# A hybrid decoder layer in 96 weight blocks: small transfers on SyncE, gate roots in the next round, later transposes and levels, another order of the last blocks

## The chip, the cores and the metric

The kernel runs on one core of a Trainium2 chip. The metric is device time in microseconds; lower is better. Names of the engines below: PE or TensorE (matmul), DVE or VectorE, ACT or ScalarE, POOL or GpSimd, SP or SyncE (here only a queue for DMAs).

## What is computed

One layer over 2064 prompt tokens (16 meta tokens in front of 2048) and 32 sample tokens (8 sequences of 4), width 1024, float32:

```python
u = rmsnorm(x, ln_mix) @ w_in                # 1024 -> 6*512: xa, ga, qb, fb, ib, gb
xc = conv_b + sum(xpad[:, j:j+T]*conv_w[j] for j in range(4))     # causal convolution of xa
r, ig = sigmoid(xc @ w_ra + b_ra), sigmoid(xc @ w_rx + b_rx)      # per head of 64
a = exp(-8 * r * softplus(-lam)); b = sqrt(1 - a*a) * ig * xc
h = scan(a*h + b);  y_a = h * gelu(ga)                            # group A
f = lb + (1-lb)*sigmoid(fb); k = (1-lb)*sigmoid(-fb); q = silu(qb)/sqrt(128); v = ib
S_t = f_t * S_{t-1} + k_t v_t^T ; o_t = q_t S_t                   # group B, 4 heads, in chunks
y_b = rms(o) * gn * silu(gb)
x = x + concat(y_a, y_b) @ w_out
x = x + square(relu(rmsnorm(x, ln_mlp) @ w_up)) @ w_down          # 1024 -> 4096 -> 1024
y = rmsnorm(x, ln_final)
```

The outputs are y and the new states (h, the last three xa, S) of the prompt and of each sample sequence.

## The kernel before

Everything lies transposed: features on the 128 partitions, tokens along the columns. The tokens are cut into two **passes** (p = 0, 1) of 1024 and 1072 columns; the second holds 1040 prompt columns and the 32 of the samples. A pass is cut into tiles of columns (`TILES`): two of 512 in pass 0, three of 358, 358 and 356 in pass 1. The weights are 96 **blocks** of 1024 x 128, kept split in two float32r parts, w_hi (rounded by ScalarE, `round_weights`) and w_lo = w_st - w_hi (by GpSimd's `split` or by VectorE, L1438). Two blocks are on chip at a time (slot = block mod 2). In pass 0 SyncE loads each block and stores its parts to DRAM (`load`, `keep`), in pass 1 GpSimd's queue loads the parts back (`reload`, L448, L449).

A **unit** is one block by one tile: 8 row blocks x 3 matmuls (w_hi a_hi, w_hi a_lo, w_lo a_hi; L481 to L483) into one of four PSUM banks (`bank`). VectorE reads the bank out and frees it. Blocks 0 to 19 are the four heads' V, G, XA, F, Q (one head is a **round**), 20 to 23 are GA, 24 to 31 OUT (the output projection), 32 to 95 the MLP. The activations are split likewise: `turn` makes a_hi (ScalarE) and a_lo (VectorE, L1189) of the mixer's output for OUT.

In blocks 0 to 23 each unit is issued in two halves; a half is a **slot** of `schedule(p)`. A round of pass 0 has 20 slots, of pass 1 30; the last round, over GA, has 16 and 24. Behind a slot's half unit every engine runs the **pieces** that the tables give that slot, mostly for the head before (i-1), each in the same order in its own queue:

- VT, KT: transposes of v and k. D and L1 to L7: products inside a chunk at distance levels; VectorE multiplies q and k by decays between levels (`merge`, L1151 to L1154), places results by mask. U: state updates. O: outputs of the head; R, N: the reciprocal and the scaling of its norm; OT: transposes back; Y: times gate, into `xy`. OT opens aux PSUM banks (four, numbered in turn by `AUX`), as do the others.
- GATE: products for r and ig and ScalarE's sigmoids, exp, tanh. GA: VectorE's u, a, v, igx from them, and ScalarE's square root of v. GB: VectorE's product with the root and the scan (L1297 to L1306).
- RS: the sums of squares of the input, its root and reciprocal (L1122). No bank can be read out before it. NF, FN, FY: the final norm of pass 0's output, run within pass 1's first round. TURN: `turn` of an early tile.

ScalarE issues the small transfers of a pass (`load_small`: masks, h0, convolution history; `load_state`) before its first slot, the state stores and loads within O, small outputs at the end of the rounds, and the loads of the residual x. VectorE waits for the small transfers before RS. OUT's first `SIDE` = 4 units run their first six row blocks, then their last two (the last heads are ready last). At the end, `FINAL_ORDER` puts blocks 94 and 95 (rows m = 6, 7) by tile: (6,0) (7,0) (6,1) (7,1) (6,2) (7,2); `last_sum` adds the residual and squares, `final_sum` sums a tile over partitions on TensorE, `finish_tile` inverts (L1122) and scales its eight row blocks (L1132), and SyncE stores them.

Of the kernel before, what the change touches and what calls it, by code (L numbers as in the profile page):

```python
# [35 lines left out]
HEADS = 4  # L36
# [27 lines left out]
SIDE = 4  # L64
# [21 lines left out]
def y_no(p, t, n):  # L86
# [7 lines left out]
               + [(m, t) for t in range(NT[1]) for m in (KB - 2, KB - 1)]]  # L94
# [37 lines left out]
def s_at(p, i, name):  # L132
# [18 lines left out]
def schedule(p):  # L151

    out = []
    for i in range(HEADS + 1):
        blks = [5 * i + b for b in range(5)] if i < HEADS else [GA0 + c for c in range(4)]
        s = 0
        for blk in blks:
            for t in range(NT[p]):
                for half in range(2):
# [5 lines left out]
                    if i >= 1 and s in SLOTS[p]:  # L165
                        pieces.append((SLOTS[p][s], i - 1))
                    if i < HEADS and s == GATE_SLOT[p]:
                        pieces.append(("GATE", i))
# [11 lines left out]
def aux_uses(p, name):  # L180

    if name in ("FN", "FY", "R", "N", "Y", "GA", "GB", "TURN"):
        return 0
    if name in ("RS", "N2", "NF"):
        return NT[p]
    if name == "GATE":
        return 2 * NT[p]
# [22 lines left out]
AUX = number_aux()  # L210


def build(nc, ins, outs):
# [6 lines left out]
    with ExitStack() as ctx:  # L220
# [170 lines left out]
        def _(sync):  # L391
# [10 lines left out]

            load(0, 0)
# [7 lines left out]
            sync.dma_start(w_rx[:, :, :], wrx_d).then_inc(const_in, 16)  # L411
            with sync.Fori(0, BLOCKS // 2 - 1) as i:
                for j in range(2):
                    sync.wait_ge(w_ready, 2 * i + (j + 1))
                    load(2 * i + (2 + j), j)
                    keep(2 * i + j, j)
            for j in range(2):
                sync.wait_ge(w_ready, BLOCKS - 1 + j)
                keep(BLOCKS - 2 + j, j)
            for t, (c0, w) in enumerate(KEPT[1]):  # L420
# [5 lines left out]
        def _(pool):  # L426
# [13 lines left out]
            for j in range(2):  # L440
                split(j, j)
# [22 lines left out]
        def _(pe):  # L464
# [40 lines left out]
            def piece(p, name, i):  # L505
# [115 lines left out]
                elif name == "GATE":  # L621
# [3 lines left out]
                    for t, (c0, w) in enumerate(TILES[p]):  # L625
                        for g, wt in enumerate((w_ra, w_rx)):
                            ps = open_bank(a + 2 * t + g)
# [8 lines left out]
            for p in range(2):  # L636
                nt = NT[p]

                for it, blk, t, half, pieces in schedule(p):
# [8 lines left out]
                    for name, i in pieces:  # L648
                        if name not in ("FN", "FY", "R", "N", "Y", "GA", "GB", "TURN"):
# [8 lines left out]
                for m, t in units[:SIDE]:  # L658
# [64 lines left out]
            for m, t in FINAL_ORDER[1][-2 * NT[1]:]:  # L723
# [4 lines left out]
                if t and m == KB - 2:  # L728
                    final_sum(1, t - 1)
# [5 lines left out]
        def _(act):  # L735
# [44 lines left out]

            def load_small(p):

                for b in range(P // BLK):
                    r_ = slice(BLK * b, BLK * (b + 1))
                    act.dma_start(mask[r_, 0:BLK], mask_d[0:BLK, 0:BLK]).then_inc(smp_in, 16)
                    act.dma_start(mask[r_, BLK:].rearrange("p (l j) -> p l j", j=HALF),
                                  mask_d[0:BLK, P:P + 64 * (DIRECT - 1)].rearrange(
                                      "p (l j) -> p l j", j=64)[:, :, 0:HALF]).then_inc(smp_in, 16)
                if p == 0:
                    return  # L790
                for g, (s0, w) in enumerate(blocks(NCH)):
                    act.dma_start(smask[s0:s0 + w, :], smask_d[s0:s0 + w, SGRP * g:SGRP * (g + 1)]).then_inc(smp_in, 16)
                act.dma_start(h0[:, :, :], h0_d).then_inc(smp_in, 16)
                act.dma_start(spad[:, :, :, 0:TAPS - 1], cs_d).then_inc(smp_in, 16)

            def load_state(i):
                act.dma_start(s_smp[:, :, :], ss_d[i]).then_inc(s_load, 16)
# [33 lines left out]
            def piece(p, name, i):  # L831
# [7 lines left out]
                elif name == "FY":  # L839
                    act.wait_ge(y_out, i + 1)  # L840
                    store(0, i, META, TH[0] - META)
# [47 lines left out]
                elif name == "O":  # L889
# [13 lines left out]
                    if p and i + 1 < HEADS:  # L903
                        act.wait_ge(s_step, s_at(p, i, "smul"))
                        load_state(i + 1)
                    if p:
                        for s in (3, 4):
                            drained(act, AUX[(p, "U", i)] + s)
                        act.dma_start(ssn_d[i], tmp[:, :, :]).then_inc(s_store, 16)
# [11 lines left out]
                elif name == "GATE":  # L921
# [3 lines left out]
                    for t, (c0, w) in enumerate(TILES[p]):  # L925
                        for g, (dst, b) in enumerate(((ta, "b_ra"), (ig, "b_rx"))):
                            u = a + 2 * t + g
                            filled(act, u)
                            fn(dst[:, c0:c0 + w], aux[u % 4][:, 0:w], ACT.Sigmoid,
                               bias=col(b, i)).then_inc(aux_free[u % 4], 1)  # L930
                    for t in range(NT[p]):
                        drained(act, a + 2 * t)
# [3 lines left out]
                elif name == "GA":  # L936
# [38 lines left out]
            for p in range(2):  # L975
# [675 lines left out]
```

## Time and profile before

| | |
|---|---|
| median of 3 runs | 2451.21 us (2449.23 to 2453.65) |
| profiled execution | 2453.71 us, its span 2451.8 us |
| PE busy | 2385.6 us, 97% of the span |
| DVE, ACT, POOL busy | 38%, 26%, 12% |
| mean granted TensorE clock | 0.988 |
| chain that ended last | PE 87%, DVE 7%, issue 3%, ACT 2% |

The span is the time from the first to the last instruction in the profiled execution; 1.9 us lie around it. A wait is idle time of an engine, put down to what ended it. Pass 0's projections run up to about 375 us, its OUT blocks to about 476, its MLP to about 1175; pass 1's projections to about 1576.

### The profile page before, as it was taken

Reading aid. Unit: us, or ns where it says so; the run is one execution under the profiler, and the core shown is the slowest. Engines: PE = TensorE matmul, PEld = TensorE weight load, DVE = VectorE, ACT = ScalarE, POOL = GpSimd, SP = SyncE. Lnnn points to the kernel's source line nnn. Section 1 sums busy time; section 2 is a strip of 40 time slices with the busy share of each in tenths; the row PEclk is TensorE's granted clock in tenths of the full one; section 3 lists DMA queues with packets and bytes.
Section 4 is the critical chain, followed back from the end, with each engine's and each line's share of the span. In section 5 each row is a group of like instructions: output and inputs, shape, how many; then the busy total and the mean of one; then the engine's idle time right before and its main releaser. Section 6 shows DMA issues by size and latency. Waiting matters only on the chain.

```text
span 2451.8 us, 38616 instructions
## 1 busy us (share of the span) xinstructions
PE 2385.6 (97%) x15850; PEld 2140.7 (87%) x15850; DVE 937.6 (38%) x1593; ACT 645.6 (26%) x1207; POOL 287.1 (12%) x276
## 2 busy tenths in 40 slices
PE   7999998999999999999999999999999999999996
PEld 5777776888888888888898899999999999999996
DVE  6766664421121121223775665544212212211224
ACT  5345343331131121222334234422201201200211
POOL 0000002222122221222000000000001000010000
PEclk9999998999999999999999999999999999999998
DMA  5332324344434444454432222332222322222223
GB/s 200 106 112 100 107 96 175 133 155 147 153 132 153 141 141 154 134 200 156 126 109 70 70 70 87 120 122 86 86 86 89 99 87 86 86 90 98 86 86 106
DMA packets 88178, 284.39 MB, mean 116 GB/s; under 512 B 15872, under 2 KB 19072, under 8 KB 88064
## 3 DMA queue, kind: packets, MB, share of 16 engines
q1 hardware_dynamic: 46512, 158.09, 18.7%
q0 software_dynamic: 27648, 100.68, 12.3%
q10 hardware_dynamic: 13904, 23.95, 2.8%
q8 instruction: 90, 1.47, 0.2%
q14 instruction: 24, 0.20, 0.0%
HBM read 171.06 MB, written 111.62 MB: 115 GB/s over the span
## 4 chain that ended last, share of the span: by engine, by line
PE 87%; DVE 7%; issue 3%; ACT 2%; ACTq 1%; DMA 0%; POOL 0%; DVEq 0%; POOLq 0%
PE bank L481 27%; PE bank L483 27%; PE bank L482 27%; PE aux L628 1%; PE aux L548 1%; DVE a_lo L1197 1%; DVE xc L1380 1%; ACT s_in L737 1%; PE aux L577 1%; PE aux L600 1%; PE aux L599 1%; ACT w_hi L737 0%; DVE xy L1306 0%; DVE rs L1141 0%; DVE xy L1132 0%
## 5 line engine op out<-in xcount | busy, mean ns | idle before, releaser
L481 PE MATMUL bank<-a_hi,w_hi 128*128 128x358 f32 (+3 forms) x2560 | 924.1, 361 | 32.1 <-DVE a_lo L1197 11.3
L482 PE MATMUL bank<-a_lo,w_hi 128*128 128x358 f32 (+3 forms) x2560 | 907.2, 354 | 0.0
L483 PE MATMUL bank<-a_hi,w_lo 128*128 128x358 f32 (+3 forms) x2560 | 907.2, 354 | 0.0
L481 PEld LDWEIGHTS bank<-a_hi,w_hi 128*128 128x128 f32 x2560 | 486.3, 190 | 84.5 <-POOL w_lo L436 19.0
L483 PEld LDWEIGHTS bank<-a_hi,w_lo 128*128 128x128 f32 x2560 | 486.9, 190 | 43.6
L482 PEld LDWEIGHTS bank<-a_lo,w_hi 128*128 128x128 f32 x2560 | 486.8, 190 | 42.7 <-issue 1.5
L481 PE MATMUL bank<-b_hi,w_hi 128*128 128x358 f32 (+3 forms) x1280 | 450.2, 352 | 0.0
L482 PE MATMUL bank<-b_lo,w_hi 128*128 128x358 f32 (+3 forms) x1280 | 449.2, 351 | 0.0
L483 PE MATMUL bank<-b_hi,w_lo 128*128 128x358 f32 (+3 forms) x1280 | 449.0, 351 | 0.0
L1508 DVE TENSOR_TENSOR xy<-xy,bank 128x356 f32 (+6 forms) x160 | 94.0, 588 | 556.1 <-PE bank L483 556.1
L737 ACT ACTIVATE a_hi<-tmp 128x356 f32 (+5 forms) x160 | 88.3, 552 | 817.3 <-DVE tmp L1498 817.3
L436 POOL TENSOR_TENSOR w_lo<-w_st,w_hi 128x1024 fp32r<-128x1024 f32 x74 | 183.8, 2484 | 975.8 <-ACT w_hi L737 975.8
L483 PEld LDWEIGHTS bank<-b_hi,w_lo 128*128 128x128 f32 x1280 | 240.8, 188 | 20.7
L482 PEld LDWEIGHTS bank<-b_lo,w_hi 128*128 128x128 f32 x1280 | 240.3, 188 | 20.7 <-issue 0.2
L481 PEld LDWEIGHTS bank<-b_hi,w_hi 128*128 128x128 f32 x1280 | 240.3, 188 | 19.9 <-issue 0.2
L1498 DVE SCALAR_TENSOR_TENSOR tmp<-bank,rs 128x356 f32<-128x356 f32 (+2 forms) x160 | 94.6, 591 | 332.1 <-PE bank L483 331.2
L448 POOL DMA_DIRECT2D w_hi<-kept_hi x96 | 50.9, 530 | 1139.2 <-PE bank L483 1139.2
L737 ACT ACTIVATE w_hi<-w_st 128x1024 fp32r<-128x1024 f32 x96 | 100.8, 1050 | 276.5 <-PE bank L483 267.9
L1501 DVE TENSOR_TENSOR a_lo<-tmp,a_hi 128x356 f32 (+5 forms) x160 | 95.1, 595 | 197.9 <-ACT tmp L737 197.9
L737 ACT ACTIVATE tmp<-tmp 128x356 f32<-128x356 f32 (+2 forms) x160 | 85.7, 536 | 0.0
L737 ACT ACTIVATE tmp<-xy 128x496 f32<-128x496 f32 (+2 forms) x75 | 40.8, 544 | 147.3 <-DVE xy L1508 147.1
L737 ACT ACT_TABLE_LOAD x57 | 73.1, 1283 | 6.5 <-issue 5.5
(166 smaller groups left out, 1407.5 us busy)
## 6 DMA issues: line engine op xcount, KB each, us to landing
w_st<-in_wall SPq DMA_DIRECT2D x96, 512.0 KB, 4.1
kept_hi<-w_hi SPq DMA_DIRECT2D x96, 512.0 KB, 4.9
kept_lo<-w_lo SPq DMA_DIRECT2D x96, 512.0 KB, 5.7
w_hi<-kept_hi POOLq DMA_DIRECT2D x96, 512.0 KB, 3.8
w_lo<-kept_lo POOLq DMA_DIRECT2D x96, 512.0 KB, 4.6
xs<-in_xT ACTq DMA_DIRECT2D x8, 536.0 KB, 7.7
xy<-in_xT ACTq DMA_DIRECT2D x8, 536.0 KB, 8.3
xy<-in_xT ACTq DMA_DIRECT2D x8, 512.0 KB, 8.2
```

Source lines behind the costliest of these rows:

```text
L436: pool.tensor_tensor(w_lo[:, slot, :], w_st[:, slot, :], w_hi[:, slot, :].bitcast(F32), ALU.subtract).then_inc(w_ready, 1)
L448: pool.dma_start(w_hi[:, slot, :], kept_hi[m]).then_inc(w_again[slot], 16)
L481: pe.matmul(ps, wh, xh, start=(j == 0), stop=False)
L482: pe.matmul(ps, wh, xl, start=False, stop=False)
L483: mm = pe.matmul(ps, wl, xh, start=False, stop=(j == 7))
L548: mm = pe.matmul(ps[s0:s0 + w, HALF * c:HALF * (c + 1)], k[:, at:at + w], right_halves(q, at, w, x), start=True, stop=True)
L577: mm = pe.matmul(ps[:, j * P:(j + 1) * P], k_tok[0:r_, c + j, :], v_tok[0:r_, c + j, :], start=True, stop=True)
L599: pe.matmul(out, q[:, lo_:hi_], s_in[:, c + j, :], start=True, stop=False)
L737: return nc.scalar.activation(out, in_, func, **kw)
L1498: stt(z, bank[lu % 4][:, 0:w], 0.0, rs[:, c0:c0 + w], ALU.max, ALU.mult).then_inc(bank_free[lu % 4], 1)
L1501: tt(a_lo[:, 4 * qd + j, c0:c0 + w], z, a_hi[:, 4 * qd + j, c0:c0 + w].bitcast(F32), ALU.subtract).then_inc(h_ready, 1)
L1508: tt(x, x, bank[lu % 4][:, 0:w], ALU.add).then_inc(bank_free[lu % 4], 1)
```

## The change

- SyncE gets `load_small`, `load_state`, the state stores, the small outputs, the stores of pass 0's output (FY) and, in pass 1, the loads of the residual x. `load_small(0)` stands before SyncE's weight loop, all else after it.
- A new piece GS holds ScalarE's square root of v, at slot 0 of the next round; GB stays at slot 0 (pass 0) and 1 (pass 1). GA goes from slot 27 to 28 in pass 1.
- Pass 0: L1 to N one slot later (D stays), OT from 14 and Y from 15 both to 16, GATE from 16 to 15, RS from 7 to 6. Pass 1: OT from 21 and Y from 22 both to 25; GATE's first two tiles from slot 24 to 23, its third as GATE2 at 24; NF, FN, FY three slots later. In the last round OT and Y are at 15 (pass 0) and 22, 23 (pass 1).
- GpSimd splits blocks 0 to 4 instead of 0 and 1; VectorE splits 5 to 23 instead of 2 to 23.
- `SIDE` is 3 in pass 0. `round_weights(25)` comes before `turn` of the second tile.
- The last blocks run (6,0) (6,1) (7,0) (7,1) (6,2) (7,2), and the final sums and scalings are placed anew.

The diff, cut to its core; its hunks are in the order constants, SyncE, GpSimd, ScalarE, VectorE.

```diff
-SIDE = 4
+SIDE = [3, 4]
+DVE_FIRST = 5
...
-               + [(m, t) for t in range(NT[1]) for m in (KB - 2, KB - 1)]]
+               + [(KB - 2, 0), (KB - 2, 1), (KB - 1, 0), (KB - 1, 1), (KB - 2, 2), (KB - 1, 2)]]
+SUM_AT = {(KB - 1, 1): 0, (KB - 2, 2): 1}
...
-SLOTS = [dict(zip(range(16), PIECES)),
-         dict(zip([0, 4, 5, 6, 8, 9, 10, 12, 13, 14, 15, 16, 18, 19, 21, 22], PIECES))]
-GATE_SLOT = [16, 24]
-GATE_A_SLOT, GATE_B_SLOT = [18, 27], [0, 1]
+AT = [[0, 1] + list(range(3, 15)) + [16, 16],
+      [0, 4, 5, 6, 8, 9, 10, 12, 13, 14, 15, 16, 18, 19, 25, 25]]
+AT_LAST = [AT[0][:-2] + [15, 15], AT[1][:-2] + [22, 23]]
+GATE_SLOTS = [{15: "GATE"}, {23: "GATE", 24: "GATE2"}]
+GATE_TILES = [{"GATE": [0, 1]}, {"GATE": [0, 1], "GATE2": [2]}]
+GATE_A_SLOT, GATE_ROOT_SLOT, GATE_B_SLOT = [18, 28], [0, 0], [0, 1]
...
-RS_SLOT = [7, 1]
-FINAL_SLOTS = {6: ("NF", 0), 7: ("FN", 0), 8: ("FN", 1), **{10 + b: ("FY", b) for b in range(8)}}
+RS_SLOT = [6, 1]
+FINAL_SLOTS = {9: ("NF", 0), 10: ("FN", 0), 11: ("FN", 1), **{13 + b: ("FY", b) for b in range(8)}}
...
+            load_small(0)
             with sync.Fori(0, BLOCKS // 2 - 1) as i:
...
+            sync.wait_ge(unit_done, unit_no(0, BLOCKS - KB, 0))
+            load_small(1)
+            sync.wait_ge(x_acc, 2 * KB)
+            sync.wait_ge(x_ready, tile_no(1, NT[1] - 1, KB - 1))
+            load_state(0)
+            for b in range(KB):
+                sync.wait_ge(y_out, b + 1)
+                sync.dma_start(y_d[b, :, META:TH[0]], xy[:, b, META:TH[0]]).then_inc(stored, 16)
+            for i in range(HEADS):
+                for s in (3, 4):
+                    drained(sync, AUX[(1, "U", i)] + s)
+                sync.dma_start(ssn_d[i], tmp[:, :, :]).then_inc(s_store, 16)
+                if i + 1 < HEADS:
+                    filled(sync, AUX[(1, "O", i)] + 2)
+                    sync.wait_ge(s_step, s_at(1, i, "smul"))
+                    load_state(i + 1)
+            sync.wait_ge(rg_step, rg_at(1, 3, "ncs"))
...
-            for j in range(2):
-                split(j, j)
+            for n in range(DVE_FIRST):
+                split(n % 2, n)
...
-                elif name == "GA":
+                elif name == "GS":
                     act.wait_ge(rg_step, rg_at(p, i, "v"))
                     fn(ea[:, 0:TH[p]], ea[:, 0:TH[p]], ACT.Sqrt, scale=-1.0).then_inc(rg_act, 1)
...
-                turn(p, NT[p] - 1, range(EARLY))
                 if p == 0:
                     round_weights(OUT0 + 1)
+                turn(p, NT[p] - 1, range(EARLY))
...
-                    if p == 0 and 0 < blk < OUT0 - 1 and t == 0 and half == 0:
+                    if p == 0 and DVE_FIRST - 1 <= blk < OUT0 - 1 and t == 0 and half == 0:
...
-                if t and m == KB - 2:
-                    finish_tile(t - 1, range(3))
-                elif t and m == KB - 1:
-                    finish_tile(t - 1, range(3, KB))
+                if (m, t) == (KB - 1, 1):
+                    finish_tile(0, range(5))
+                elif (m, t) == (KB - 2, 2):
+                    finish_tile(0, range(5, KB))
+            finish_tile(1, range(KB))
             finish_tile(NT[1] - 1, range(KB))
```

## Rows read from the trace of the kernel before

**Rows 1.** The page, part 5, groups: busy us, mean ns of one | idle before.

```profile
L436 POOL TENSOR_TENSOR w_lo<-w_st,w_hi 128x1024 fp32r<-128x1024 f32 x74 | 183.8, 2484 | 975.8 <-ACT w_hi L737 975.8
...
L737 ACT ACT_TABLE_LOAD x57 | 73.1, 1283 | 6.5 <-issue 5.5
```

**Rows 2.** Waits of TensorE over the span: us in total, times, longest.

```profile
PE aux L619 <- ACT s_in L737: 9.3, 13, 2.3
PE bank L481 <- POOL w_lo L436: 7.1, 2, 4.0
PE bank L481 <- DVE v L1340: 6.2, 1, 6.2
PE aux L498 <- ACT rs L737: 5.1, 1, 5.1
PE aux L498 <- DVE gate L1531: 4.6, 2, 3.3
PE bank L481 <- DMA w_lo<-kept_lo: 3.8, 1, 3.8
PE aux L548 <- DVE q L1216: 2.4, 4, 0.6
...
PE bank L481 <- DVE w_lo L1438: 2.0, 1, 2.0
PE bank L481 <- DVE a_lo L1189: 1.8, 2, 1.1
```

**Rows 3.** Stretches of TensorE: us, PE busy (count), granted clock, DMA share, GB/s.

```profile
41.44:48.27 6.83, 4.96 (x12) 0.50 0.55 200
386.19:393.02 6.83, 5.85 (x14) 0.50 1.02 390
...
430.00:436.83 6.83, 6.83 (x32) 1.00 0.44 176
1195.14:1201.97 6.83, 4.75 (x12) 0.50 0.53 85
1314.61:1318.02 3.41, 3.41 (x13) 0.50 0.02 5
1399.94:1406.77 6.83, 6.64 (x23) 0.50 0.00 0
...
1700.00:1706.83 6.83, 6.83 (x44) 1.00 0.39 134
2410.29:2417.12 6.83, 5.55 (x19) 0.50 0.01 3
```

**Rows 4.** Timeline of ScalarE and VectorE, start of pass 0: start us, us, instruction [idle before].

```profile
32.95 0.34 ACTq L785 DMA_DIRECT2D mask<-in_mask  x1
...
36.77 1.06 ACT L737 ACTIVATE w_hi<-w_st 128x1024 fp32r<-128x1024 f32 x1 [5.33 <-issue]
...
39.10 3.35 DVE L1122 RECIPROCAL rs<-rs 128x512 f32<-128x512 f32 x1
```

**Rows 5.** Timeline of TensorE and GpSimd at OUT; of VectorE late in pass 0.

```profile
383.69 0.40 PE L483 MATMUL bank<-a_hi,w_lo 128*128 128x512 f32 x1
387.17 0.78 PE L481 MATMUL bank<-a_hi,w_hi 128*128 128x496 f32 x1 [3.08 <-POOL w_lo L436]
...
381.04 6.08 POOL L436 TENSOR_TENSOR w_lo<-w_st,w_hi 128x1024 fp32r<-128x1024 f32 x1 [12.42 <-ACT w_hi L737]
...
1160.67 1.10 DVE L1531 TENSOR_TENSOR gate<-gate,tmp 128x496 f32<-128x496 f32 x1 [0.69 <-ACT tmp L737]
...
1171.58 0.68 DVE L1531 TENSOR_TENSOR gate<-gate,tmp 128x496 f32<-128x496 f32 x1 [0.68 <-ACT tmp L737]
```

**Rows 6.** Timeline of TensorE and VectorE, start of pass 1.

```profile
1191.12 0.99 PE L498 MATMUL aux<-gate,ones 128*128 128x496 f32 x2
...
1198.20 2.39 DVE L1122 RECIPROCAL rs<-rs 128x358 f32<-128x358 f32 x1 [10.37 <-DMA spad<-in_conv]
```

**Rows 7.** Timeline of VectorE, last instructions of the kernel.

```profile
2444.83 4.09 DVE L1132 SCALAR_TENSOR_TENSOR xy<-xy,par,gate 128x356 f32<-128x356 f32 x8
```

More of the change, by code:

```diff
@@ L164, in schedule @@
                         pieces.append(("RS", 0))
[L165 to L168, printed above, removed]
+                    if i >= 1 and s == GATE_ROOT_SLOT[p]:
+                        pieces.append(("GS", i - 1))
+                    if i >= 1:
+                        at = (AT if i < HEADS else AT_LAST)[p]
+                        pieces += [(name, i - 1) for name, slot in zip(PIECES, at) if slot == s]
+                    if i < HEADS and s in GATE_SLOTS[p]:
+                        pieces.append((GATE_SLOTS[p][s], i))
                     if i < HEADS and s == GATE_A_SLOT[p]:
@@ L185, in aux_uses @@
         return NT[p]
-    if name == "GATE":
-        return 2 * NT[p]
+    if name in ("GATE", "GATE2"):
+        return 2 * len(GATE_TILES[p][name])
     if name == "D" or name[0] == "L":
@@ L210, with gate_aux @@
 AUX = number_aux()
+def gate_aux(p, i, t):
+    name = "GATE" if t < 2 else "GATE2"
+    return AUX[(p, name, i)] + 2 * (t % 2)
 def build(nc, ins, outs):
@@ L401, in load_x0, with load_small, load_state @@
                 sync.dma_start(xs[:, b, c0:c0 + w], xT[b, :, c0:c0 + w]).then_inc((x_in2 if t else x_in)[b], 16)
+            def load_small(p):
+                for b in range(P // BLK):
+                    r_ = slice(BLK * b, BLK * (b + 1))
+                    sync.dma_start(mask[r_, 0:BLK], mask_d[0:BLK, 0:BLK]).then_inc(smp_in, 16)
+                    sync.dma_start(mask[r_, BLK:].rearrange("p (l j) -> p l j", j=HALF),
+                                  mask_d[0:BLK, P:P + 64 * (DIRECT - 1)].rearrange(
+                                      "p (l j) -> p l j", j=64)[:, :, 0:HALF]).then_inc(smp_in, 16)
+                if p == 0:
+                    return
+                for g, (s0, w) in enumerate(blocks(NCH)):
+                    sync.dma_start(smask[s0:s0 + w, :], smask_d[s0:s0 + w, SGRP * g:SGRP * (g + 1)]).then_inc(smp_in, 16)
+                sync.dma_start(h0[:, :, :], h0_d).then_inc(smp_in, 16)
+                sync.dma_start(spad[:, :, :, 0:TAPS - 1], cs_d).then_inc(smp_in, 16)
+            def load_state(i):
+                sync.dma_start(s_smp[:, :, :], ss_d[i]).then_inc(s_load, 16)
             load(0, 0)
@@ L620, in piece @@
                         mm.then_inc(aux_done, 1)
-                elif name == "GATE":
+                elif name in ("GATE", "GATE2"):
                     if n == 0:
@@ L657, in _ @@
                 units = [(m, t) for m in range(KB) for t in range(nt)]
-                for m, t in units[:SIDE]:
+                for m, t in units[:SIDE[p]]:
                     if t == 0:
@@ L662, in _ @@
                     out_unit(m, t, range(EARLY))
-                for m, t in units[:SIDE]:
+                for m, t in units[:SIDE[p]]:
                     out_unit(m, t, range(EARLY, KB))
-                for m, t in units[SIDE:]:
+                for m, t in units[SIDE[p]:]:
                     if t == 0:
@@ L779, in input_squares @@
                     input_square(p, b)
[L781 to L797, printed above, removed]
             def rms_tile(p, a, dst, t, tiles):
@@ L920, in piece @@
                     turn(p, i, range(EARLY))
-                elif name == "GATE":
+                elif name in ("GATE", "GATE2"):
                     if i > 0:
@@ L1463, in _ @@
                     for name, i in pieces:
-                        if name not in ("RS", "NF", "GATE"):
+                        if name not in ("RS", "NF", "GATE", "GATE2", "GS"):
                             piece(p, name, i)
```

71 lines of the change are left out of this document (30 added, 41 removed).

## The prediction

> **What bounds the kernel now.** I read the page first, then the waits of TensorE, then its low-clock stretches by the timeline, then the timelines of the other engines around each long wait. TensorE is busy 97% of the span and its matmuls are the same in both kernels: the products of w_hi, w_lo with the activations, plus the small ones of the heads. So only three things can move the time: waits of TensorE, stretches in which its clock is granted at 1.2 instead of 2.4 GHz, and the tail after its last product. [Rows 2] names the waits: nearly all are single events at seams (start of a pass, last projection round, OUT products, end) or recur once in each head's round. [Rows 3] shows the stretches at half clock; each begins in or right behind a wait of 2 us and more. Their price comes from the counts: at full clock a 512-column product starts every 6.83/30 = 0.23 us (32 are counted, two lie over the ends), a 358-column one every 6.83/42 = 0.16; in the slow stretches 5.85/14 = 0.42 and 5.55/19 = 0.29. So a product in such a stretch costs 0.19 us more in pass 0 and 0.13 more in pass 1 [rows 3]. A wait costs more than its printed idle time as well: the last product before the wait at 387.17 starts at 383.69, 3.48 later stands the next, against 0.23 usual, so 3.25 are lost where 3.08 are printed [rows 5]: 0.17 more for each wait.
>
> **Start of pass 0** (small transfers to SP, `RS` one slot earlier, GpSimd splits blocks 0 to 4). Before, ScalarE issues eight mask transfers from 32.95 on and rounds block 2's weights only at 36.77; the square roots and VectorE's reciprocal, at 39.10, stand behind [rows 4], and TensorE waits 6.2 us for the V read-out [rows 2]. On SP the eight issues, 3.8 us (36.77 - 32.95), come before its loop, where SP's next need, the third weight load, isn't wanted by ScalarE before about 33: hidden; if not, it is the same 3.8. Rounding then starts at about 32.95, and TensorE's sums of squares can run there too (the same x_acc releases both; TensorE, a half unit earlier in its order, waits there for about 0.5). The w_lo split leaves VectorE too, so the reciprocal starts at about 34.8 and the bank comes free 4.4 earlier: 1.8 of the 6.2 stay. The slow stretch of 12 products goes: 12 x 0.19 = 2.3. Term: 4.4 + 2.3 = **6.7**. The later wait of 2.0 for VectorE's w_lo (L1438, behind convolution and `rest_of_prep`) goes, as GpSimd makes block 4's half: its 2.48 us [rows 1] have most of a block's products, 48 x 0.23 = 11 us, as cover. Term: **2.0**.
>
> **The rounds of pass 0.** Levels stand a half unit later behind D. L1 waited for D's VectorE work 2.4 us in four waits [rows 2]; the extra half unit is 12 x 0.23 = 2.8 us: gone. The gate roots (`GS`) go from slot 18 to the next round's slot 0. Before, ScalarE stood at slot 18 until VectorE had v, with every later instruction behind it; now its root, about as long as a rounding of that width (1.06, [rows 4]; an estimate), and a table load of 1.28 [rows 1] stand in front of V's copies, and VectorE's `GB` (product and scan) waits for them with its bank read-outs queued behind. I bound this between -1.3 (one table switch less before the round) and +2.3 us on VectorE's side; near zero is likeliest, as the root moves past one sigmoid only, and the 2.8 of the shifted levels covers either end. Term: **2.4**.
>
> **The transposes of OT, both passes.** They waited 9.3 us in 13 waits, the longest 2.3 [rows 2]: in pass 1 the norm N sits behind the convolution on VectorE and arrives at its slot late. Now OT comes two slots after N in pass 0 (5.6 us) and six after it in pass 1 (six half units, 12 us, against two). All 9.3 go. The three slow stretches behind them, 13, 23 and again 13 products (the third, at 1488.69, is as the first), go with them: 49 x 0.13 = 6.4. Term: **15.7**. OT now opens aux banks that the gates just used; TensorE waits there if ScalarE's sigmoids lag. `GATE2` splits the pass-1 set so that four products, not six, come at once, with a half unit between: bounds 0 to 1 us a round in pass 1, taken 0.3.
>
> **OUT of pass 0.** Two waits for GpSimd's w_lo, 7.1 in all, and 0.7 of the 1.8 for a_lo L1189 [rows 2]. The first w_lo took 6.08 us [rows 5] against 2.48 on average [rows 1], while VectorE ran its a_lo subtractions back to back. Moved ahead of `turn`, the rounding ends about 1.1 earlier than the first a_hi, so GpSimd starts before that run. Its mirror image is in the trace: with a split in flight, VectorE's subtraction-like tensor_tensor at 1160.67 takes 1.10 where the same at 1171.58 takes 0.68 [rows 5]. So whoever starts first keeps the other out: w_lo of block 25 takes 2.5 and is in time, the first a_lo of the second tile comes about 1.4 late, of which the shift of the last round (OT no longer ahead of the last products) hides half. I leave 0.8 of wait. That is the reading of the Trainium skill, page "SBUF — State Buffer", section "SBUF: two separate sides", too: the port pair shared by VectorE and GpSimd is an exclusive lock that the first to start keeps for its whole instruction; the trace agrees by 1.10 against 0.68. SIDE = 3 puts unit (1,1) whole, 24 x 0.23 = 5.5 us, between the end of block 24 and the use of block 26, in place of two quarter units (2.8): the 4.0 wait goes. Both slow stretches, 14 products each (the second one at 406.67 is like the first), go: 28 x 0.19 = 5.3. Term: 7.1 + 0.7 - 0.8 + 5.3 = **12.3**. If GpSimd is starved once more, as in the row of 6.08, w_lo comes 1.9 late and a slow stretch follows: 12.3 - 4 = 8.
>
> **Start of pass 1.** ScalarE issued twelve small transfers and the state load before the square roots; VectorE's reciprocal waited 10.4 us for the last to land [rows 6] and TensorE 5.1 for the root [rows 2]. On SP they follow the last `keep`, 20 us ahead. The reciprocal can then start at 1187.9 (1198.20 - 10.37), TensorE has products for its fourth bank until 1191.12 at least and half a unit more with NF out of the way, and the first bank is free by 1187.9 + 2.4 + 0.5 (a read-out, about as wide as a scaling) = 1190.8 [rows 6]: no wait. NF to slot 9 keeps aux banks out of it. Slow stretch: 12 x 0.13 = 1.6. Term: **6.7**. What is late next is VectorE, with two reciprocals, eight output scalings (now slots 13 to 20) and the convolution before gate slot 23: I allow 0 to 2 us, in the small waits below.
>
> **End of pass 1's rounds.** ScalarE issues five small outputs before the third `turn`; on SP they cost it nothing. The 1.1 left of a_lo L1189 goes: **1.1**. SP is idle there; its queue holds state stores, state loads and residual loads in the order in which they fall due, half a round and more ahead of each use: nothing.
>
> **The end.** Block 95's reload is 3.8 us late [rows 2], with a slow stretch of 19 x 0.13 = 2.5 behind. The new order puts (6,1) in front of (7,0): 24 x 0.16 = 3.9 us of cover, just enough (0 to 0.3 stays). Of the 4.6 for the last sums the first, 1.3, goes too. With 0.17 for each restart TensorE ends 8 us earlier. But all eight scalings of tile 1 and its reciprocal now come after the last sum, where five stood: 2.4 + 3 x 0.51 = 3.9 more on VectorE (0.51 = 4.09/8, [rows 7]). Term: 8.2 - 3.9 = **4.3**.
>
> **Sum.** 6.7 + 2.0 + 2.4 + 15.7 + 12.3 + 6.7 + 1.1 + 4.3 = 51.2. Restarts: 23 waits outside the tail x 0.17 = 3.9. New small waits (gates, VectorE's load, a table load at the wrong place): -2.6, taken between 0 and 6. Together -52.5 us. The profiled span of 2451.8 becomes 2399.3; that run took 2453.7, 2.5 above the median of 2451.2, so the run would be 2401.2 and the median 2451.2 - 52.5 = **2398.7 us**.
>
> **Rivals.**
> (a) Waits shrink below what is printed but clock stretches stay at several seams, since a rest of 1 to 2 us is left there: start, OUT and two of the rounds, 2.3 + 5.3 + 3.4 plus their rests of 4: 2411 to 2414. For it: 1.8 and 0.8 are left by my own sum. Against: waits of 2.0 (L1438) and 1.1 had no slow stretch behind them.
> (b) OT's new place moves the wait instead of removing it (the change doesn't do what it says): TensorE then waits for ScalarE's gate sigmoids by as much as it did for N. Term 15.7 lost: 2414.
> (c) The roots at the round's start are on the path: a table load and root, 2.3, per round, with a slow stretch of 1.7 to 2.5 behind: seven rounds x 4 to 4.8 = 28 to 34: 2427 to 2433.
> (d) Slower than before: the same place, but VectorE, waiting in GB, holds its read-outs until all four banks are full. A round then loses the root, the covered 2.8 of the levels, and up to a unit (5.5 in pass 0) with its slow stretch: about 10 us, x 7 = 70: 2469. It decides against the change from 57/7 = 8.2 us a round. Against it: four banks are three units of slack, 12 to 16 us.
>
> **How the numbers follow.** My forecast, 0.76: 2390 to 2408. (a) 0.12, (b) 0.05, (c) 0.03, (d) 0.02, and 0.02 for other small gains or none. The range of 8 in 10 takes the forecast's bounds and reaches into (a) and (b): 2388 to 2416. Faster by over 0.2% (about what a measurement of this kernel can tell from no change, 5 us): 0.96; within: 0.02; slower: 0.02.
>
> **What would show it.** TensorE's waits without L1438, the q of L1216, POOL w_lo, DMA w_lo, and s_in; the clock granted in full at 1195, in the rounds of pass 1 and near the last blocks; GpSimd's second OUT split near 2.5 us and VectorE's first a_lo beside it longer than 0.6; ScalarE without DMA issues at both pass starts; the last sum near 8 us earlier relative to block 89's end and 13 us of VectorE behind it. I'd be wrong if aux L619 or L628 waits for ScalarE's sigmoids, if VectorE waits for ea in GB with TensorE idle, or if new waits of over 2 us stand at the seams.

## The result, and the profile after

The changed kernel takes 2426.68 us (median of 4 runs, 2424.64 to 2428.21) against 2452.43 of the kernel before (4 runs, 2449.23 to 2453.84): ratio 0.9896, 95% interval 0.9879 to 0.9913. The direction was right, the size was half of the forecast: 25.7 us less where 52.5 were predicted, and 2426.68 lies above the range of 2388 to 2416. The profiled execution took 2426.67, its span is 2425.0 (before 2451.8), so the two traces differ by 26.8.

The page of the kernel after, its head and parts 1 and 4:

```profile
span 2425.0 us, 38626 instructions
...
PE 2375.2 (98%) x15850; PEld 2137.6 (88%) x15850; DVE 936.9 (39%) x1590; ACT 642.7 (27%) x1207; POOL 291.7 (12%) x279
...
PE 93%; DVE 3%; ACT 1%; issue 0%; DVEq 0%; ACTq 0%
```

Its waits of TensorE, the view of [rows 2]: us in total, times, longest. Line numbers have moved: L540 to L542 are the products (L481 to L483 before), L658 the product of O, L607 the levels, L594 D, L557 the sums of squares, L1209 `turn` of the mixer's output (L1189).

```profile
PE aux L658 <- DVE s_in L1274: 14.4, 4, 4.7
PE bank L540 <- DVE a_lo L1217: 11.1, 1, 11.1
PE bank L540 <- DVE a_lo L1209: 3.1, 1, 3.1
PE aux L557 <- DVE gate L1550: 2.8, 1, 2.8
PE aux L607 <- DVE q L1236: 1.9, 1, 1.9
PE bank L540 <- DVE v L1359: 1.5, 1, 1.5
PE aux L594 <- DVE q L1374: 1.2, 1, 1.2
```

Gone are both w_lo waits of GpSimd, w_lo of L1438, the late reload, rs, all 13 of s_in from ScalarE (OT) and 4.7 of the 6.2 for v. The 11.1 is the first load of the kernel, before any product; the kernel before has it too. The first line is new and the largest: O waits for VectorE's state update U. The wait for a_lo of L1209 has grown: 3.1 in one, where two came to 1.8. On the page PE's busy time fell by 10.4 us (fewer products at half clock) and its share of the last chain rose from 87 to 93%.

The rows that answer [rows 4] and [rows 6], timeline of ScalarE and VectorE in the kernel after, starts of pass 0 and pass 1 (start us, us, instruction, idle before):

```profile
32.96 1.06 ACT L797 ACTIVATE w_hi<-w_st 128x1024 fp32r<-128x1024 f32 x1 [1.51 <-DVE rs L1161]
...
35.29 3.35 DVE L1142 RECIPROCAL rs<-rs 128x512 f32<-128x512 f32 x1 [2.37 <-ACT rs L797]
...
1188.14 2.39 DVE L1142 RECIPROCAL rs<-rs 128x358 f32<-128x358 f32 x1
```

Block 2's rounding is 3.8 us earlier (36.77 before), the reciprocal also (39.10 before; the prediction said 34.8), and pass 1's reciprocal no longer waits for a transfer.

Stretches of TensorE in the kernel after, the view of [rows 3]: length, busy time and count of PE, PEld, DVE, ACT, POOL, then the granted clock, DMA share and GB/s.

```profile
129.77:136.60 6.83, 5.65 (x26) 5.65 (x27) 2.40 (x5) 1.14 (x8) 0.00 (x0) 0.50 0.43 118
211.69:218.52 6.83, 6.11 (x28) 6.11 (x29) 2.04 (x4) 1.14 (x8) 0.00 (x0) 0.50 0.49 145
293.61:297.02 3.41, 2.93 (x13) 2.94 (x14) 1.83 (x3) 0.00 (x0) 0.00 (x0) 0.50 0.17 16
389.18:396.01 6.83, 6.14 (x15) 4.83 (x16) 5.93 (x10) 2.73 (x6) 0.00 (x0) 0.50 0.81 249
1180.00:1186.83 6.83, 6.83 (x39) 6.19 (x37) 6.70 (x15) 5.75 (x13) 0.00 (x0) 1.00 0.16 57
1532.65:1536.06 3.41, 3.41 (x15) 3.41 (x14) 2.79 (x5) 0.00 (x0) 0.00 (x0) 0.50 0.02 5
```

The stretch at the start of pass 1 (1180) now has the full clock, as predicted. Three new ones at 1.2 GHz stand in the rounds of pass 0, each from the last 0.5 to 1.2 us of one of O's waits on. One stands at the wait for a_lo (before, two at OUT), and one, at 1532.65, has no wait in front of it.

**Where the 26.8 went.** I took each product's start minus the start of the product before it, less the median of that spacing for the same pair of shapes, and summed the excess over each stage. That counts waits, what they cost beside their printed time, and slow stretches alike.

| stage | before | after | moved | forecast |
|---|---|---|---|---|
| start of pass 0 (to 60 us) | 10.7 | 4.7 | -6.0 | -6.7 |
| rounds of pass 0 (60 to 370) | 24.3 | 39.0 | **+14.8** | -6.6 |
| OUT of pass 0 | 14.5 | 6.4 | -8.1 | -12.3 |
| start of pass 1 | 7.4 | 0.7 | -6.7 | -6.7 |
| rounds of pass 1 | 28.8 | 13.5 | -15.3 | -14.6 |
| last blocks, to TensorE's end | 11.6 | 3.3 | -8.3 | -8.2 |
| from there to the kernel's end | 11.3 | 14.6 | +3.3 | +3.9 |

The forecast of 15.7 for OT is for both passes. Of the 9.3 us of its waits, seven (0.2 to 0.4 each, 2.2 in all) stood in pass 0, so 2.2 of it stand with the rounds of pass 0 (2.4 + 2.0 + 2.2 = 6.6) and 13.5 with those of pass 1. The stages sum to 26.3 (forecast 51.2, and 1.3 more for restarts less new small waits). One stage holds 21.4 of the miss of 26.2, OUT 4.2; the other stages are within 0.7 each.

**The new wait.** Timeline of VectorE in the kernel after, second round of pass 0 with an earlier head in it:

```profile
203.17 0.69 DVE L1359 TENSOR_TENSOR xpad<-bank,rs 128x512 f32<-128x512 f32 x1 [4.55 <-PE bank L542]
...
205.01 3.92 DVE L1399 SCALAR_TENSOR_TENSOR xc<-xpad,par,xc 128x1024 f32<-128x1024 f32 x3
208.97 0.23 DVE L1262 COPY s_in<-state 128x128 f32<-128x128 f32 x1
209.30 3.05 DVE L1274 SCALAR_TENSOR_TENSOR s_in<-s_in,f,aux 128x128 f32<-128x128 f32 x7
...
212.41 0.80 PE L658 MATMUL aux<-s_in,q 128*128 128x128 f32 x2 [4.71 <-DVE s_in L1274]
```

And VectorE at the same place of the kernel before:

```profile
206.19 0.35 DVE L1254 SCALAR_TENSOR_TENSOR state<-s_in,f,aux 128x128 f32<-128x128 f32 x1
206.69 0.69 DVE L1340 TENSOR_TENSOR xpad<-bank,rs 128x512 f32<-128x512 f32 x1 [0.15 <-PE bank L483]
...
208.54 3.93 DVE L1380 SCALAR_TENSOR_TENSOR xc<-xpad,par,xc 128x1024 f32<-128x1024 f32 x3
```

In pass 0 XA (the third block of a round) ends with slot 11, and there VectorE runs the read-out and the whole convolution, 5.8 us from 203.17 to 208.97, ahead of the slot's pieces. Before, U stood at slot 10: its chain was done at 206.54, and the read-out at 206.69 and the convolution stood behind it. With "L1 to N one slot later" U is at slot 11, behind the convolution, and O at slot 12 asks for it one half unit later. The last round projects GA and has no XA. U and O are at slots 11 and 12 there too, and O's wait is 0.2 us. That is a control inside the same trace:

```profile
369.74 0.49 PE L658 MATMUL aux<-s_in,q 128*128 128x128 f32 x2 [0.20 <-DVE s_in L1274]
```

### The profile page after: what moved, and what is told of

Read it like the earlier page. It is cut to its first block, busy times and chain, and to the rows that moved or that the text cites. A ratio compares the mean times of both kernels' runs of the same rounds, so it can differ in the third digit from the quotient of the medians.

```text
span 2425.0 us, 38626 instructions
## 1 busy us (share of the span) xinstructions
PE 2375.2 (98%) x15850; PEld 2137.6 (88%) x15850; DVE 936.9 (39%) x1590; ACT 642.7 (27%) x1207; POOL 291.7 (12%) x279
## 4 chain that ended last, share of the span: by engine, by line
PE 93%; DVE 3%; ACT 1%; issue 0%; DVEq 0%; ACTq 0%
PE bank L540 29%; PE bank L542 29%; PE bank L541 29%; PE aux L607 1%; PE aux L688 1%; PE aux L658 1%; PE aux L659 1%; DVE xc L1399 0%; DVE xy L1152 0%; DVE s_in L1274 0%; PE aux L613 0%; PE aux L636 0%; PE aux L557 0%; PE aux L626 0%; DVE gate L1142 0%
## 5 line engine op out<-in xcount | busy, mean ns | idle before, releaser
L540 PE MATMUL bank<-a_hi,w_hi 128*128 128x358 f32 (+3 forms) x2560 | 919.4, 359 | 15.8 <-DVE a_lo L1217 11.1
L542 PE MATMUL bank<-a_hi,w_lo 128*128 128x358 f32 (+3 forms) x2560 | 902.5, 353 | 0.0
L540 PEld LDWEIGHTS bank<-a_hi,w_hi 128*128 128x128 f32 x2560 | 482.1, 188 | 64.7 <-POOL w_lo L495 11.4
L542 PEld LDWEIGHTS bank<-a_hi,w_lo 128*128 128x128 f32 x2560 | 483.2, 189 | 43.3
L540 PE MATMUL bank<-b_hi,w_hi 128*128 128x358 f32 (+3 forms) x1280 | 450.2, 352 | 0.0
L542 PE MATMUL bank<-b_hi,w_lo 128*128 128x358 f32 (+3 forms) x1280 | 449.0, 351 | 0.0
L542 PEld LDWEIGHTS bank<-b_hi,w_lo 128*128 128x128 f32 x1280 | 240.8, 188 | 20.6
L540 PEld LDWEIGHTS bank<-b_hi,w_hi 128*128 128x128 f32 x1280 | 240.2, 188 | 19.9 <-issue 0.2
```

What stands on the lines that cost most here:

```text
L540: pe.matmul(ps, wh, xh, start=(j == 0), stop=False)
L542: mm = pe.matmul(ps, wl, xh, start=False, stop=(j == 7))
```

## The experiments

My theory (A) was: the new place of U and O behind XA's convolution costs some 22 us, three waits with their slow stretches; the rest of the miss lies at OUT. The rival (B): the loss hangs on the levels' shift or the moved roots as such, not on the convolution. Runs of e1 to e4 share one set of runs of before (median 2451.18), e5 to e8 a second (2450.65), e9 and e10 a third (2451.73).

**e4: the kernel before, with the level shift alone.**

```diff
-SLOTS = [dict(zip(range(16), PIECES)),
-         dict(zip([0, 4, 5, 6, 8, 9, 10, 12, 13, 14, 15, 16, 18, 19, 21, 22], PIECES))]
+AT = [[0, 1] + list(range(3, 15)) + [15, 15],
+      [0, 4, 5, 6, 8, 9, 10, 12, 13, 14, 15, 16, 18, 19, 21, 22]]
...
```

> The kernel before with one part of the change alone: L1 to N of pass 0 one slot later (OT and Y at 15), nothing else. Theory A: three waits of O of about 4.7 us appear with slow stretches behind, less the 2.4 us of L1's waits: about 19 us above the kernel before's 2452.4, 2471. Theory B: the shift alone does no harm, 2449 to 2453.

Measured: 2464.67 us, ratio 1.0058 (1.0041 to 1.0074), 13.5 us slower. Its waits of TensorE:

```profile
PE aux L599 <- DVE s_in L1254: 14.4, 4, 4.7
...
PE aux L619 <- ACT s_in L737: 6.8, 6, 2.0
```

The three waits and three stretches at half clock (133.76, 215.68, 297.60) come with this edit alone, and L1's waits go. So one part of the change, by itself, costs 13.5 us. I expected 19. My sum had counted only L1's 2.4 as a gain. The traces have more: pass 0's seven waits of OT (2.2), the four for k (0.9) and one of 0.8 are gone as well, 3.9 in all (OT too is one slot later here). That leaves 1.6 of the 5.5, about what a restart of 0.17 for each of these twelve waits makes (2.0).

**e2: the changed kernel, with the convolution of a round that has pieces put behind the slot's pieces.**

```diff
-                            convolve(p, un[0])
+                            if p == 0 and un[0] > 0:
+                                late = un[0]
+                            else:
+                                convolve(p, un[0])
...
+                    if late is not None:
+                        convolve(p, late)
```

> The changed kernel, all slots as changed, but in pass 0's second to fourth round VectorE runs the convolution behind the pieces of slot 11 (behind U) instead of ahead of them. Theory A: the three O waits fall below 0.5 us and the slow stretches in these rounds go, 22 us below the changed kernel: 2405; the gates' wait for the convolution stays hidden (their slot is 15). Theory B (roots at the round's start): U still comes late, gain under 3 us, 2424 or more. Theory C (moving the convolution only hands the wait on to GATE or to bank read-outs): O's waits go, as long ones of L688 or of L540 appear, 2415 to 2427.

Measured: 2403.24 us, 0.9811 (0.9795 to 0.9828), 23.4 less than the changed kernel. VectorE in that slot:

```profile
195.26 0.69 DVE L1359 TENSOR_TENSOR xpad<-bank,rs 128x512 f32<-128x512 f32 x1 [4.55 <-PE bank L542]
195.86 0.22 DVE L1262 COPY s_in<-state 128x128 f32<-128x128 f32 x1
196.20 3.07 DVE L1274 SCALAR_TENSOR_TENSOR s_in<-s_in,f,aux 128x128 f32<-128x128 f32 x7
199.37 0.35 DVE L1274 SCALAR_TENSOR_TENSOR state<-s_in,f,aux 128x128 f32<-128x128 f32 x1
```

The convolution follows; O's waits fall from 14.4 to 0.2 us, and all slow stretches between 60 and 360 us are gone. The levels and roots stand where the change put them, so (B) falls. No new wait of the gates (L688) or for a bank appears, so the wait isn't handed on (theory C). The two profiled executions are 24.6 us apart. By the excess of each product, 22 of it lie in these rounds: 14.6 of waits (3 x 4.88) and 7.3 in the three slow stretches. Most of the rest are a shorter stretch at OUT (3.41 for 6.83 us, 1.3) and the stretch at 1532.65, which e2's trace lacks (some 1.6); these two aren't the convolution's.

**e1: the levels back, the rest of the change kept.**

```diff
-AT = [[0, 1] + list(range(3, 15)) + [16, 16],
+AT = [list(range(14)) + [16, 16],
```

> The changed kernel with the pieces L1 to N of pass 0 back in their old slots (levels 2 to 8, KT 9, U 10, O 11, R 12, N 13); all else as changed. Theory A: the new 4.9 us waits of O for VectorE's s_in come from U standing in slot 11, in which VectorE convolves first, and from nothing else: the three waits (14.4 us) and their three slow-clock stretches (about 7) go, the waits of L1 for D's q (2 to 3 us in all) come back: about 19 us below the changed kernel's 2426.7, 2408. Theory B: VectorE is late in every round because the gate roots stand at the round's start: the O waits stay with L1 back, 2424 to 2428.

Measured: 2423.25 us, 0.9891 (0.9874 to 0.9907): (A) as I then had it, 2408, fell. O's waits and their stretches were gone, as (A) says, but the waits of TensorE have a new head:

```profile
PE aux L607 <- DVE q L1236: 12.6, 4, 4.7
```

The timelines of VectorE and TensorE at one of them show why:

```profile
165.98 1.23 DVE L1316 TENSOR_TENSOR k_tok<-k_tok,ea 128x1024 f32<-128x1024 f32 x1 [1.07 <-ACT ea L797]
167.25 2.35 DVE L1325 TENSOR_TENSOR_SCAN xy<-ta,hprev,k_tok 128x1024 f32<-128x1024 f32 x1
...
170.63 1.22 DVE L1236 TENSOR_TENSOR q<-q,f 128x1024 f32<-128x1024 f32 x1
...
171.90 0.74 PE L607 MATMUL aux<-q,k 128*32 128x16 f32 x64 [2.64 <-DVE q L1236]
```

ScalarE's root (ea) reaches `GB` 1.07 us late, behind a rounding and a table load; product and scan follow, and V's read-out and D's q stand behind them. L1 waits 2.6 in each of three rounds and 4.7 in the first, 0.6 at the longest before [rows 2]. So with the levels at their old slots VectorE's D is about 2 us later for TensorE than before. The wait for the root is 1.07 of that; what makes the rest isn't separated, since no run has both the levels and the roots at their old places. With the levels shifted these three waits are gone: the shift hides them, and the order of U and the convolution takes more than it gives.

**e3: the root back at slot 18 (28 in pass 1), the rest kept.** The piece GS is issued in the same round as GA.

> The changed kernel with the gate root back right behind GA in both passes (slots 18 and 28) instead of slot 0 of the next round. Theory A: O's waits of 4.7 us stay; the root's place is worth little: within 3 us of the changed kernel, 2424 to 2430. Theory B (roots at the round's start make VectorE late): O's waits shrink by 2 us each or go, 2405 to 2418.

Measured: 2424.59 us, 0.9893 (0.9877 to 0.991), within the spread of the changed kernel. O's waits stay at 14.4; the first round's L1 wait falls from 1.9 to 0.8, D's rises from 1.2 to 1.5. With the shift as cover the root's place is worth nothing that can be told here.

**The OUT seam.** The kernel after, timelines of VectorE, GpSimd and TensorE:

```profile
380.92 3.61 DVE L1209 TENSOR_TENSOR a_lo<-xy,a_hi 128x496 fp32r<-128x496 f32 x6 [3.06 <-ACT a_hi L797]
384.44 0.68 DVE L1359 TENSOR_TENSOR xc<-bank,rs 128x512 f32<-128x512 f32 x1
...
386.43 1.40 DVE L1302 SCALAR_TENSOR_TENSOR xy<-aux,par,gate 128x512 f32<-128x512 f32 x2
...
386.81 2.36 POOL L495 TENSOR_TENSOR w_lo<-w_st,w_hi 128x1024 fp32r<-128x1024 f32 x1 [16.95 <-ACT w_hi L797]
...
387.75 6.76 DVE L1209 TENSOR_TENSOR a_lo<-xy,a_hi 128x512 fp32r<-128x512 f32 x9
...
389.87 0.77 PE L540 MATMUL bank<-a_hi,w_hi 128*128 128x512 f32 x1 [3.10 <-DVE a_lo L1209]
```

GpSimd's split is in time (6.08 us in [rows 5], now 2.36), and VectorE's first a_lo of the second tile stands behind it: it takes 1.97 us (387.75 to 389.72), the others 0.68. Four runs on top of e2 took this apart.

*e5: the rounding of block 25 behind `turn` again.*

```diff
+                turn(p, NT[p] - 1, range(EARLY))
                 if p == 0:
                     round_weights(OUT0 + 1)
-                turn(p, NT[p] - 1, range(EARLY))
```

> The kernel of e2 (2403.2) with block 25's rounding back behind turn of the second tile. There TensorE waits 3.1 us for VectorE's first a_lo of that tile, which takes 2.0 us in place of 0.6 since GpSimd's split runs beside it. Theory L (the split and the subtractions of VectorE keep each other out, first come first): that wait falls to about 1.8 (what is left is VectorE's run on the first tile and Y), GpSimd's split takes about 6 us again and TensorE waits 3 to 3.5 for it, with the slow stretch: 2404 to 2408. Theory R (it is only ScalarE's 1.05 us rounding ahead of a_hi): the wait falls by 1.05 to 2.0 and nothing new comes: 2401 to 2402.

Measured: 2404.13 us, 0.9813 (0.9796 to 0.9829). The same instructions, GpSimd and VectorE:

```profile
367.81 6.09 POOL L495 TENSOR_TENSOR w_lo<-w_st,w_hi 128x1024 fp32r<-128x1024 f32 x1 [20.07 <-ACT w_hi L797]
...
365.62 6.06 DVE L1209 TENSOR_TENSOR a_lo<-xy,a_hi 128x512 fp32r<-128x512 f32 x10
```

The wait for a_lo falls from 3.1 to 1.8, and one of 1.5 for w_lo takes its place (I had expected 3 to 3.5): nothing gained. Rounding first costs VectorE 1.3 us (7.36 in e2 against 6.06 for ten a_lo) and gives GpSimd 3.7 (6.09 against 2.36). Of the 6.09, 2.2 lie behind the end of VectorE's run, nearly all that the split needs by itself.

*e6: the split of block 25 in four quarters of 256 columns.*

```diff
+            for c in range(4):
+                part = slice(DM // 4 * c, DM // 4 * (c + 1))
+                ins = pool.tensor_tensor(w_lo[:, 1, part], w_st[:, 1, part], w_hi[:, 1, part].bitcast(F32),
+                                         ALU.subtract)
...
```

> The kernel of e2 with GpSimd's split of block 25 cut into four instructions of 256 columns, rounding ahead of turn. Theory L (whole-instruction lock): VectorE's first a_lo gets in after one quarter, takes about 1 us in place of 2.0, and TensorE's wait for it falls from 3.1 to about 2; but the quarters left stand until VectorE's run of ten ends, so the split ends 2 us late for block 25: together no gain, 2402 to 2406. Theory R (they share bandwidth, or only the rounding counts): the split ends about 0.3 us later than in one piece, the wait for a_lo stays at 3.1, 2403 to 2404.

Measured: 2403.41 us, 0.9806 (0.9789 to 0.9822).

```profile
364.88 3.69 POOL L506 TENSOR_TENSOR w_lo<-w_st,w_hi 128x256 fp32r<-128x256 f32 x4 [16.89 <-ACT w_hi L804]
...
365.81 7.49 DVE L1216 TENSOR_TENSOR a_lo<-xy,a_hi 128x512 fp32r<-128x512 f32 x10
```

Two quarters start before VectorE's a_lo and take 0.72 and 0.73 us. The other two fall into the run and take 1.18 each, and the three a_lo beside them 1.02 to 1.22 in place of 0.68: they take turns. The wait falls to 2.2 with w_lo in time; I had expected w_lo 2 us late, which did not happen. In the median it gained nothing that can be measured.

*e7: the split of block 25 by VectorE, behind its first six a_lo; the last Y behind that.*

```diff
+                    tt(w_lo[:, 1, :], w_st[:, 1, :], w_hi[:, 1, :].bitcast(F32), ALU.subtract).then_inc(w_ready, 1)
+                    piece(0, "Y", HEADS - 1)
...
```

> The kernel of e2 with block 25 split by VectorE (after the six a_lo of the second tile, then Y of the last head), rounding behind turn, nothing on GpSimd beside them. Theory L: each a_lo takes 0.6 us, TensorE's wait at the second tile falls from 3.1 to about 0.5, block 25's weights come in time, the slow stretch goes: 3.5 to 4.5 below e2, 2399 to 2400. Theory R: VectorE as the only worker is late for w_lo instead, a wait of 1 to 2 us for it: 2402 to 2404.

Measured: 2401.94 us, 0.9797 (0.9781 to 0.9814), 1.3 below e2 with overlapping spreads (2399.52 to 2403.63 against 2402.04 to 2405.15). Six a_lo take 3.70, the wait for them is 0.5, and no slow stretch stands at the seam. But GpSimd's next split is 2.5 us late: ScalarE's roundings stand behind parts of the residual, whose loads were issued only from 370.97, once the late `turn`s had their Y.

*e9: e7, with six residual loads ahead of the late `turn`s.*

```diff
+                if p == 0:
+                    for n, b in enumerate(OUT_ORDER[:EARLY]):
+                        act.wait_ge(y_ready, y_no(p, NT[p] - 1, n))
+                        load_x(p, xy, b)
...
```

> The kernel of the run with VectorE's split of block 25, and with the first six residual loads (x into xy) issued on ScalarE ahead of the late turns of pass 0's last tile instead of behind them. There the loads were issued from 370.97 us on and ScalarE's residual part came 4.68 us late behind the landing, so GpSimd's w_lo of block 26 came 2.5 us late to TensorE at 385.98. Theory: with the loads issued some 5 us earlier that wait of 2.5 goes, TensorE's waits at the seam sum to under 1 us, and the kernel takes 2.5 to 3 us less: 2398.5 to 2399.5 us. Rival: each load needs the y of its row block, which VectorE writes only then, and ScalarE is held by that instead; the wait for w_lo of block 26 stays above 2 us and the time stays at 2401 to 2403 us.

Measured: 2400.14 us (2398.56 to 2401.13), 0.9788 (0.9772 to 0.9805). The 2.5 is gone from the waits. The excess of the seam is 1.0 us, where the changed kernel has 6.4 and e2 5.2. The time came out 1.8 lower than e7, expected 2.5 to 3, with overlapping spreads (e7's 2399.52 to 2403.63), so the time alone doesn't show a gain over e7. Its median is the lowest of the study.

**e8: e2, with pass 1's OT and Y at slots 21 and 22.**

```diff
-      [0, 4, 5, 6, 8, 9, 10, 12, 13, 14, 15, 16, 18, 19, 25, 25]]
-AT_LAST = [AT[0][:-2] + [15, 15], AT[1][:-2] + [22, 23]]
+      [0, 4, 5, 6, 8, 9, 10, 12, 13, 14, 15, 16, 18, 19, 21, 22]]
+AT_LAST = [AT[0][:-2] + [15, 15], AT[1][:-2] + [21, 22]]
```

> The kernel of e2 with OT and Y of pass 1 back in slots 21 and 22 (gates stay split over 23 and 24). If the term of the forecast holds (three rounds with waits of 2.0 to 2.3 and 0.4 us for ScalarE's norm, slow stretches of 13, 23 and 13 products behind them): 12 to 15 us above e2, 2415 to 2418. If the gates' new slots and ScalarE's smaller queue had brought N in time by themselves: under 4 us above e2, 2407 at most.

Measured: 2417.27 us, 0.9862 (0.9845 to 0.9878), 14.0 above e2. VectorE and TensorE in one round:

```profile
1273.92 3.98 DVE L1399 SCALAR_TENSOR_TENSOR xc<-xpad,par,xc 128x1040 f32<-128x1040 f32 x3
...
1279.21 0.17 DVE L1294 RECIPROCAL o_ss<-o_ss 128x8 f32<-128x8 f32 x1
...
1281.79 0.66 PE L678 MATMUL aux<-ident,s_in 128*128 128x128 f32 x4 [1.83 <-ACT s_in L797]
```

N's reciprocal waits out the convolution, as the prediction said. Pass 1's part of the term of 15.7 is 13.5, and 14.0 confirms it. Some 1.6 of the difference may be another thing: e8's trace has a stretch at 1522.24 like that at 1532.65, e2's has none.

**e10: e2, with pass 1's small transfers back on ScalarE, ahead of its roots.**

```diff
                 act.wait_ge(x_ready, tile_no(p, NT[p] - 1, KB - 1))
+                if p:
+                    load_small(1)
+                    load_state(0)
```

> The kernel with the convolution's last slot put behind (2403.2 us), with pass 1's masks, h0, convolution history and first state load back on ScalarE, ahead of its square roots at the start of pass 1. Theory, the term of the prediction for the start of pass 1: VectorE's reciprocal waits again about 10 us for the last small transfer, TensorE waits about 5 us for the root with its sums of squares, and 12 products behind that at half clock cost 1.6 us: 6.7 us, so 2409 to 2411 us. Rival, the other moves at this seam (final norm three slots later, sums one slot later) had made the room and the transfers are hidden anyway: 2403 to 2405 us, with less than 1 us of wait for rs.

Measured: 2414.20 us (2413.10 to 2414.57), 0.9846 (0.983 to 0.9863), 11.0 above e2. VectorE, ScalarE's root and TensorE:

```profile
1176.37 2.39 DVE L1158 RECIPROCAL rs<-rs 128x358 f32<-128x358 f32 x1 [10.03 <-DMA spad<-in_conv]
...
1175.04 1.46 ACT L792 ACTIVATE rs<-aux,eps 128x358 f32<-128x358 f32 x3 [11.24 <-issue]
...
1179.38 0.67 PE L535 MATMUL bank<-a_hi,w_hi 128*128 128x358 f32 x1 [7.63 <-DVE v L1375]
```

The rival (hidden anyway) falls. The transfers cost more here than the term of 6.7: the excess at this start is 9.2 above e2's (a wait of 7.6, its restart and a slow stretch). Two slow stretches of 3.41 us that e2's trace lacks, at 93.42 and 1520.19, add some 1.6 each; that accounts for the 12.5 between the two profiled executions. In the kernel before TensorE waited 5.1 for the root and had NF's products behind it; with NF at slot 9 it waits for a bank, so the reciprocal of 2.39 comes on top. That reading is argued from the rows, no run separates it.

## Why the prediction was wrong

**The step that failed** is in "The rounds of pass 0": "Levels stand a half unit later behind D" was costed for L1 alone, as a gain of 2.4, and the term left it there. But the edit moved twelve pieces (L1 to L7, KT, U, O, R, N), and each of them meets other neighbours on VectorE. The half unit on which U lands is the one with the convolution, 5.8 us in front of it; O follows one half unit (2.8 us) later. The rows were there to read: in the trace of before the read-out ahead of the convolution starts 0.15 us after U's chain ends. In place of -2.4 (and -2.0 for L1438, -2.2 for OT) this stage brought +14.8. e2, with only the order of these two turned, is 23.4 us faster, and its excess in this stage is some 8 us below that of the kernel before: the gain of 6.6 that I had forecast was there, under a cost that I had put at nothing. My list of what would prove me wrong had waits for gate sigmoids, for `ea`, and waits of over 2 us at the seams; it did not have O.

**The roots.** "Near zero is likeliest" was too low: in e1 L1 waits 2.6 in a round where 0.6 was the longest, about +2, near my upper bound of 2.3, with 1.07 of it shown to be the root's. That the 2.8 of the shift would cover either end was right but for the first round, where L1 still waits 1.9 and D 1.2; e3, with the roots back, has 0.8 and 1.5 there, so only some 0.8 of that is the roots'.

**OUT of pass 0**: -8.1 for -12.3. The lock worked as the prediction read it (split 2.36 us, in time, first a_lo delayed), and the second wait is gone (by the trace; no run undoes SIDE = 3). Mis-sized was what is left: 3.1 us of wait and its stretch of 15 products at half clock, where I left 0.8. I let the last round's shift hide half of the delay, as if VectorE's work moved ahead with TensorE's. It did not: VectorE is the later engine there, with six a_lo of the first tile (3.61 us) in front of the last read-out. e5, without the delay, still waits 1.8 for a_lo, where the kernel before waited 0.7. My fallback for OUT, 8, has the size that was measured, but by luck: its reason was a starved GpSimd. In the Trainium skill, page "SBUF — State Buffer", section "SBUF: two separate sides", the first to start keeps the shared ports for its whole instruction. The trace agrees (the first a_lo ends 0.55 us after the split and the ten take 7.36 against 6.06 us), and shows more: between ten back-to-back instructions of VectorE a GpSimd instruction of the whole block hardly gets in (6.09 against 2.36).

**Right**, by trace and run: OT in pass 1 (e8: 14.0) and the start of pass 1 (-6.7 for -6.7; e10 shows that the transfers carry it). By the trace alone, as no run undoes them: the start of pass 0 (-6.0 for -6.7; a wait of 1.5 for v where I left 1.8), the w_lo of L1438, the last blocks (-8.3 for -8.2) and the tail behind them (+3.3 for +3.9). The timeline of VectorE at the end of the kernel after shows that tail, the scalings of [rows 7] once for tile 1 and once for tile 2:

```profile
2409.62 2.38 DVE L1142 RECIPROCAL gate<-gate 128x358 f32<-128x358 f32 x1
2412.04 4.10 DVE L1152 SCALAR_TENSOR_TENSOR xy<-xy,par,gate 128x358 f32<-128x358 f32 x8
2416.06 2.37 DVE L1142 RECIPROCAL gate<-gate 128x356 f32<-128x356 f32 x1
2418.46 4.09 DVE L1152 SCALAR_TENSOR_TENSOR xy<-xy,par,gate 128x356 f32<-128x356 f32 x8
```

With both misses taken out by other means the kernel comes to the forecast: e9 takes 2400.14, against 2398.7. The measured 2426.68 lies at the lower end of rival (c), 2427 to 2433, but not by its mechanism: e3 takes the roots away from the round's start and gains nothing that can be told.

**A reading that was wrong.** The prediction says that each stretch at half clock begins in or behind a wait of 2 us and more. In the kernel before, the one at 1488.69 follows a wait of 1.83 (at 1486.56) and one of 0.38; e8 has three stretches behind waits of 1.83 too, while the wait of 1.98 for L1438 has none. So 2 us divides nothing here, and the wait of 1.8 that I left at the start of pass 0 could have had a stretch (the 1.5 that came had none).

**Open**: why the stretch at 1532.65 has half the clock. TensorE was busy all through it and just before it, with U's small products. Eight of the ten runs have a like one at the same place (e9 at 1506.85), e2 and e5 have none. A wait of 0.39 at U, a good microsecond ahead of it, stands in six of the eight and in e2 and e5 as well, so it doesn't decide it. The stretch costs some 1.6 us, and two traces can differ by that for no reason that these runs show.

## What to carry to other kernels

When a diff moves a series of pieces by one slot, cost each of them against what its engine does in the new slot, unscheduled work (read-outs, a convolution at a block's end) above all, and not only the first piece, for whose sake it is moved. A slack of one half unit between producer and consumer is used up by any single piece of work that long on the producer's engine: list those first. A move that looks free may be free only because another edit of the same change covers it; runs that undo one edit each show such pairs (e1 and e3 here). For a gain, too, list every wait in the slots that move: e4's expectation was 5.5 us off for small ones.

## What the runs showed of the hardware

- VectorE and GpSimd: a split of 128x1024 takes 2.36 us when it starts first and 6.09 when ten back-to-back subtractions of VectorE are running; cut in four it takes 3.69 at about the same cost to VectorE (7.49 against 7.36 us). Two quarters of e6 got in during VectorE's run, 1.18 us each against 0.72 for the two before them, where e5's whole split did not.
- Waits of 4.7 us in the changed kernel went with 6.83 us at 1.2 GHz twice and with 3.41 once. Behind the wait in the first round e10 (1.90) and e9 (1.95) have a slow stretch of 3.41 us, at 93.42 and 93.73; e2 (1.89) and e7 (1.95) have none. So the same wait may or may not cost a stretch, some 1.6 us for 3.41 and 2.8 to 3.0 for 6.83 here.
